# Ringless first stage, latent norms inside the projection loop and paced activation fetches in a two-block transformer kernel

## The reference, cut to what matters

```
mod = silu(c) @ w_ada + b_ada              # 48 columns of 128; the first 16 shift and scale h
h = rmsnorm(x) * (1 + sc_a) + sh_a
proj = h @ w_in                            # qa, ka, va, q_lat (256), kv_lat (128), k_rope (32)
q = rmsnorm(q_lat, q_norm) @ w_q_up        # latent attention, 8 heads
kv = rmsnorm(kv_lat, kv_norm) @ w_kv_up
...                                        # two attentions, w_out, residual
idx, g = the 16 best of 16384 experts per token and head
act = gelu(h @ expert_u[idx]);  x += g_f * sum(g * act * expert_v[idx])
```

## Time and profile before

| | us |
|---|---|
| median of 3 runs | 2427.87 (2425.49 to 2429.12) |
| profiled execution | 2450.04, span 2448.2, granted clock 0.98 |
| PE busy | 2336.0 (95%) |
| DVE, ACT, POOL busy | 1340.0, 784.0, 1079.8 |
| DMA | 409 MB, 167 GB/s over the span |

### The profile page before, as it was taken

One profiled execution on the slowest core, in us unless ns is written; L12 is line 12 of the kernel. 1 busy time (PEld: TensorE's weight loads), 2 busy tenths in 40 slices (PEclk: granted clock), 3 DMA queues, 4 the chain that ended last, 5 costly groups with the idle time before them and its releaser, 6 DMA issues. The chain is left out here.

```text
span 2448.2 us, 32933 instructions
## 1 busy us (share of the span) xinstructions
PE 2336.0 (95%) x11679; PEld 2001.3 (82%) x11679; DVE 1340.0 (55%) x2424; ACT 784.0 (32%) x1176; POOL 1079.8 (44%) x728
## 2 busy tenths in 40 slices
PE   6999998999999999999969999999999989999999
PEld 5777776888888888888759999999977767788787
DVE  5566656899763222222228888888866554333322
ACT  1344532222333222222213333333332442333211
POOL 0029653455788888884058877882100300000000
PEclk9999998999999999999979999999998999999999
DMA  6213226734577776677539999999721101223222
GB/s 249 69 55 111 80 92 232 241 129 148 126 177 197 142 145 143 148 143 214 188 117 331 349 355 357 369 345 350 287 80 48 35 18 61 86 95 99 92 88 88
DMA packets 177648, 409.03 MB, mean 167 GB/s; under 512 B 55712, under 2 KB 97568, under 8 KB 170528
## 3 DMA queue, kind: packets, MB, share of 16 engines
q1 hardware_dynamic: 115296, 315.53, 38.8%
q0 software_dynamic: 61696, 84.12, 13.4%
q10 hardware_dynamic: 576, 8.39, 1.0%
HBM read 347.00 MB, written 60.95 MB: 167 GB/s over the span
## 5 line engine op out<-in xcount | busy, mean ns | idle before, releaser
L1448 DVE TENSOR_TENSOR p_lo<-p_raw,p_hi 128x1024 fp32r<-128x1024 f32 x230 | 282.4, 1228 | 523.3 <-ACT p_hi L1347 374.4
L58 PE MATMUL ps<-p_h_hi,p_hi 128*128 128x512 f32 x1152 | 454.3, 394 | 8.2 <-DMA p_big<-keys_d 5.2
L59 PE MATMUL ps<-p_h_lo,p_hi 128*128 128x512 f32 x1152 | 449.8, 390 | 0.0
L60 PE MATMUL ps<-p_h_hi,p_lo 128*128 128x512 f32 x1152 | 449.8, 390 | 0.0
L1223 POOL DMA_INDIRECT gates<-p_tok,p_g_cell x256 | 410.5, 1603 | 78.3 <-issue 78.3
L58 PE MATMUL ps<-p_w_hi,p_hi 128*128 128x384 f32 x1024 | 347.4, 339 | 18.7 <-DVE p_w_lo L1596 14.6
L59 PE MATMUL ps<-p_w_lo,p_hi 128*128 128x384 f32 x1024 | 346.1, 338 | 4.2 <-issue 4.1
L60 PE MATMUL ps<-p_w_hi,p_lo 128*128 128x384 f32 x1024 | 346.2, 338 | 3.6 <-issue 3.6
L1347 ACT ACTIVATE p_hi<-p_raw 128x1024 fp32r<-128x1024 f32 x144 | 152.6, 1059 | 471.0 <-PE ps L60 464.9
L58 PEld LDWEIGHTS ps<-p_h_hi,p_hi 128*128 128x128 f32 x1152 | 217.4, 189 | 53.8 <-DMA p_big<-keys_d 5.3
L60 PEld LDWEIGHTS ps<-p_h_hi,p_lo 128*128 128x128 f32 x1152 | 217.0, 188 | 45.5
(11 more groups left out here) (361 smaller groups left out, 3890.8 us busy)
## 6 DMA issues: line engine op xcount, KB each, us to landing
p_raw<-U_d SPq DMA_DIRECT2D x128, 512.0 KB
p_raw<-V_d SPq DMA_DIRECT2D x128, 512.0 KB
a_w_raw<-w_ada_d SPq DMA_DIRECT2D x48, 512.0 KB, 3.9
activations<-p_q SPq DMA_DIRECT2D x128, 192.0 KB
f_raw<-w_gu_d SPq DMA_DIRECT2D x44, 512.0 KB, 3.5
gates<-p_dense POOLq DMA_DIRECT2D x16, 1024.0 KB, 8.2
p_big<-activations SPq DMA_DIRECT2D x8, 1536.0 KB
p_h_lo<-activations SPq DMA_DIRECT2D x8, 1536.0 KB
```

Of the source, the lines that this page charges most:

```text
L58: pe.matmul(out, w_hi, x_hi, start=start, stop=False)
L59: pe.matmul(out, w_hi, x_lo, start=False, stop=False)
L60: return pe.matmul(out, w_lo, x_hi, start=False, stop=stop)
L1448: dve.tensor_tensor(lo[:, r % 2, :], raw[:, r, :], hi[:, r % 2, :].bitcast(F32), ALU.subtract).then_inc(lo_ready, 1)
```

## The change

It has three parts. (1) First stage: the 16 `w_ada` blocks have places of their own in buffers that are free until later (`qh`, `kh`, `v_mla`, `q_swa`, `o_tok`), so SP waits for none of them. Seven blocks are raw, the last among them; nine are folded, and for five of these (`ADA_SCALED`) ACT makes the product with eight activations of 128x128, so that DVE only adds. PE's order is written out by hand, with the sums of squares after raw block 4; DVE inverts after its sixth fold; ACT's root stands behind the last scaled block. (2) The latent norms: sums after blocks KROPE and Q0, inverses at K and Q0+1, roots at K and Q0+1, the normed latents at Q0+2 and Q0+3, the key copy at Q0+1; `keep_awake(60)` goes. (3) peer: cells are fetched in groups of 8 with a ring of 4 groups; the first 16 are paced, two for each V tile; V tiles 4 and 5 are loaded before `group(1, 1)`.

```diff
-    ADA_RAW = [1, 4, 7, 9, 12, 14]
-    ADA_FOLD = [m for m in range(ADA_A) if m not in ADA_RAW]
+    ADA_RAW = [0, 2, 4, 9, 11, 14, 15]
+    ADA_FOLD = [1, 3, 5, 7, 6, 8, 10, 12, 13]
+    ADA_SCALED = [6, 8, 10, 12, 13]
+    SUMS_BY = 6
...
@@ sync
-                stream.loads(sp, 0, 2)
-                sp.dma_start(xT[:], xT_d).then_inc(x_loaded, 16)
-                stream.loads(sp, 2, 4)
+                for m in range(2):
+                    ada_load(m)
...
+                for m in range(2, 4):
+                    ada_load(m)
+                sp.dma_start(xT[:], xT_d).then_inc(x_loaded, 16)
+                for m in range(4, 10):
+                    ada_load(m)
+                stream.loads(sp, 0, 2)
+                for m in range(10, ADA_A):
+                    ada_load(m)
+                stream.loads(sp, 2, 4)
...
@@ gpsimd
-                pool.wait_ge(silu_done, 1)
+                pool.wait_ge(mod_step, 1)
...
@@ tensor
-                for m in ADA_RAW:
-                    ada(m)
+                ada(0)
+                ada(2)
                 pe.wait_ge(ones_in, 16)
+                column(0)
+                column(1)
+                keep_awake(pe, ps[:, 4, :], ones[:], 8)
+                ada(4)
                 for k in range(KD):
                     pe.wait_ge(norms.sq_ready, k + 1)
                     pe.matmul(norms.bank, ones[:], x_square(k), start=k == 0, stop=k == KD - 1).then_inc(norms.summed, 1)
-                for a, m in enumerate(ADA_FOLD):
-                    keep_awake(pe, ps[:, 4, :], ones[:], 2)
...
+                column(2)
+                column(3)
+                ada(9)
+                column(4)
+                column(5)
+                ada(11)
+                ada(14)
+                column(6)
+                ada(15)
+                for a in range(7, len(ADA_FOLD)):
+                    column(a)
                 keep_awake(pe, ps[:, 4, :], ones[:], 12)
...
-                    if j == K:
+                    if j == KROPE:
                         norms.sums(pe, ones[:], 1, KD, 2)
-                    if j == Q0 + 2:
-                        norms.sums(pe, ones[:], 2, KD + 2, 1)
...
-                keep_awake(pe, ps[:, 4, :], ones[:], 60)
+                    if j == Q0:
+                        norms.sums(pe, ones[:], 2, KD + 2, 1)
@@ scalar
+                def scale(b):
+                    m = ADA_SCALED[b]
+                    act.wait_ge(ada_in[m], 16)
+                    if b >= 2:
+                        act.wait_ge(multiplied, b - 1)
+                    for k in range(KD):
+                        ins = act.activation(scaled_w[b % 2][:, k, :], by_k(ada_w[m])[:, k, :], ACT.Copy, scale=cact[:, k:k + 1])
+                    ins.then_inc(prod_ready, 1)
...
+                scale(0)
+                scale(1)
                 stream.split_hi(act, 0)
                 stream.split_hi(act, 1)
+                scale(2)
+                scale(3)
+                scale(4)
                 norms.root(act, 0)
...
-                    if j == V:
+                    if j == K:
                         norms.root(act, 1)
+                    if j == Q0 + 1:
                         norms.root(act, 2)
+                    if j == Q0 + 2:
                         normed.act(act, KD, latn_hi, 2)
+                    if j == Q0 + 3:
                         normed.act(act, KD + 2, latn_hi[:, 2:3, :], 1)
+                    if j == Q0 + 1:
                         act.wait_ge(rotation.done, 1)
                         act.activation(kh[HD:MLA_QK, :, :], k_rope[HD:MLA_QK, :]...).then_inc(shared, 1)
@@ vector (the fold loop: a scaled block has the three adds alone; then)
+                    if a == SUMS_BY - 1:
+                        norms.inverse(dve, 0, KD, D)
...
-                    if j == Q0:
+                    if j == K:
                         norms.inverse(dve, 1, KD + 2, 2 * P)
-                    if j == V:
+                    if j == Q0 + 1:
                         norms.inverse(dve, 2, KD + 3, P)
+                    if j == Q0 + 2:
                         dve.wait_ge(norms.rstd_ready, 2)
...
+                    if j == Q0 + 3:
                         dve.wait_ge(norms.rstd_ready, 3)
...
@@ peer
-    FETCH = 16
+    FETCH, FETCH_RING = 8, 4
...
+                for t in range(4, 6):
+                    v_load(t, t % 4)
                 sp.wait_ge(projected, BLOCKS)
                 group(1, 1, True)
-                for t in range(4, 2 * GT):
+                for t in range(6, 2 * GT):
...
                 def fetch_cell(s):
+                    if s % FETCH == 0 and s // FETCH >= FETCH_RING:
+                        pool.wait_ge(slot_ready, s // FETCH - FETCH_RING + 1)
...
                 for s in range(2 * FETCH):
+                    if s % 2 == 0:
+                        pool.wait_ge(lo_ready, V0 + s // 2 + 1)
                     fetch_cell(s)
```

More of the change, by code:

```diff
@@ L89, in __init__ @@
         self.pooled = []
-        self.folded = []
         for n, (kind, _, _) in enumerate(items):
-            {"split": self.where, "raw": self.raws, "pooled": self.pooled, "folded": self.folded}[kind].append(n)
+            {"split": self.where, "raw": self.raws, "pooled": self.pooled}[kind].append(n)
     def wait_landed(self, eng, n):
@@ L588, in mixer1 @@
     QLAT, KVLAT, KROPE, K, Q0, V, UPQ, UPK, UPV, OUT = 0, 2, 3, 4, 5, 9, 10, 18, 22, 26
-    ADA_RAW = [1, 4, 7, 9, 12, 14]
-    ADA_FOLD = [m for m in range(ADA_A) if m not in ADA_RAW]
+    ADA_RAW = [0, 2, 4, 9, 11, 14, 15]
+    ADA_FOLD = [1, 3, 5, 7, 6, 8, 10, 12, 13]
+    ADA_SCALED = [6, 8, 10, 12, 13]
+    SUMS_BY = 6
     ADA_POOL = list(range(ADA_A, 48))
[L594 to L597, removed]
+    items = [("split", w_in_d[m], SLOT) for m in range(10)]
     items += [("split", w_q_up_d[m], SLOT) for m in range(2)] + [("split", w_kv_up_d, SLOT)]
@@ L627, in mixer1 @@
                                                             sem("ada_done"))
+        ada_in = [sem(f"ada_in{m}") for m in range(ADA_A)]
+        raw_done, multiplied, prod_ready = sem("raw_done"), sem("multiplied"), sem("prod_ready")
         fold_step, fold_ready, fold_done = sem("fold_step"), sem("fold_ready"), sem("fold_done")
@@ L634, in mixer1, with by_k @@
         k_pads = [k_swa[:], o_tok[:, 1, 1, :]]
-        fold = qh[:, 0:2, :].rearrange("p a (k c) -> p (a k) c", c=P)
-        folded = qh[:, 2:5, :].rearrange("p a (k c) -> p (a k) c", c=P)
+        ada_w = [h[:, 2 * i:2 * i + 2, :] for h, n in ((qh, 4), (kh, 4), (v_mla, 2), (q_swa, 2)) for i in range(n)]
+        ada_w += [o_tok[:, i // 2, 2 * (i % 2):2 * (i % 2) + 2, :] for i in range(4)]
+        def by_k(block):
+            return block.rearrange("p a (k c) -> p (a k) c", c=P)
+        fold = by_k(normed.full[:])
+        scaled_w = [product[:], by_k(normed.x[:])]
+        folded = [h[:, c * P:c * P + P] for h in (k_swa[:], v_swa[:].rearrange("p t c -> p (t c)")) for c in range(4)]
+        folded += [partial[:, c, :] for c in range(2)]
         ss = sb("ss", [P, 2 * TT])
         def x_square(k):
-            return o_tok[:, k // TT, k % TT, :]
+            return norms.sq[:, k, :] if k < 2 else rotation.x[:, k - 2, :] if k < 4 else rotation.t[:, (k - 4) // 2, k % 2, :]
         square = rotation.t[:, 1, 1, :]
@@ L669, in _, with ada_load @@
             def _(sp):
+                def ada_load(m):
+                    sp.dma_start(ada_w[m], w_ada_d[m].rearrange("p (a n) -> p a n", a=2)).then_inc(ada_in[m], 16)
                 sp.dma_start(cols[:], cols_d).then_inc(cols_in, 16)
-                stream.loads(sp, 0, 2)
-                sp.dma_start(xT[:], xT_d).then_inc(x_loaded, 16)
-                stream.loads(sp, 2, 4)
+                for m in range(2):
+                    ada_load(m)
                 o, w = TABS["ones"]
                 sp.dma_start(ones[:], tabs_d[:, o:o + w]).then_inc(ones_in, 16)
-                stream.loads(sp, 4, ADA_A + 2)
+                for m in range(2, 4):
[7 more added lines that the diff above has]
+                stream.loads(sp, 2, 4)
                 sp.dma_start(sink[:], sink_d).then_inc(loaded, 16)
@@ L680, in _ @@
                     sp.dma_start(dst[:], tabs_d[:, o:o + w]).then_inc(loaded, 16)
-                stream.loads(sp, ADA_A + 2)
+                stream.loads(sp, 4)
             @block.gpsimd
@@ L712, in ada, with column @@
                         return
-                    n = stream.raws[ADA_RAW.index(m)]
-                    stream.wait_landed(pe, n)
+                    pe.wait_ge(ada_in[m], 16)
                     for k in range(KD):
-                        mm = pe.matmul(ps[:, 6, m:m + 1], stream.raw[:, n % stream.R, k * P:k * P + P], cact[:, k:k + 1],
+                        mm = pe.matmul(ps[:, 6, m:m + 1], by_k(ada_w[m])[:, k, :], cact[:, k:k + 1],
                                        start=(k == 0), stop=(k == KD - 1))
-                    mm.then_inc(stream.raw_used, 1)
```

(39 more changed lines are left out.)

8 lines of the change are left out of this document (3 added, 5 removed).

## The result

The changed kernel takes 2400.49 us (median of 4 runs, 2394.37 to 2404.01) against 2426.68 (2413.72 to 2429.12) for the kernel before: ratio 0.99, 95% interval 0.9859 to 0.9942. It is 26 us faster. The time lies inside the range, 28 us above the forecast; the gain is a little less than half of the 55 that were summed. The profiled execution takes 2404.01, span 2402.2.

The account below looks back on a forecast made before the run. PE was taken to bound the kernel, busy 95% of the span, partly with useless matmuls, and waiting at V's start. 15 + 13 + 27 = 55 off the profiled 2450.0 gives 2395, less 22.2 gives 2373; range 2362 to 2402.

Parts of the forecast that it names:

- The median of the runs is 22.2 lower; the same difference gives 2373: Whole kernel: profiled 2450.0 less 55 gives 2395; the profile-to-median difference of 22.2 was then subtracted to reach 2373.
- Part 1: First stage: PE still sets its end, first useful matmul moves from 61.92 to 46.8; gain 15, bounds 21 and 7.
- Part 2: Latent norms in the projections: 15.7 + 2 - 3 - 1 - 1 = 13 gained; bounds 16 and 5.
- waits before V: Projections: inverse at Q0+1, then ACT's root and key copy, delay block V's inputs; a new PE wait of about 3.
- the wait before block 5: Projections, at 96.81: ACT was held in the third square; with the sums one block earlier the wait goes, gaining 2.
- Behind V the third latent and the last split take 1 more: Projections, between block V and UPQ: finishing the latents was charged as a loss of 1.
- Part 3: Start of V: 29.1 lost up to tile 7's end; pacing cells recovers all but 2; gain 27, bounds 31 and 0.
- Rival 1: Start of V: the stall comes from entering loops, not the cells; gain 28 + 0 to 4, about 2398; chance 0.17.
- what is late is its code: Start of V: matmuls inside a tile wait for no semaphore, so PE's waits of up to 1.77 are for late code.
- Rival 2: Early norms become waits of 3 each at K, Q0+1, Q0+2; total gain 47, 2381; chance 0.16 shared with Rival 3.
- Rival 3: First stage: PE fills it, unloading DVE is beside the path; gain 7 there, total 47, 2381; 0.16 shared with Rival 2.
- Rival 4: V: rows come late because POOL sets the pace above 3.84 a pair; 99 lost at 5.0, about 2440; chance 0.04.

Follow-up runs that it names:

- A: Comparison on one chip: kernel before 2453.02, again 2453.92; only the peer edits 2426.08; changed kernel with peer as before 2435.06; 64 cells at once 2496.31.
- C: Comparison on another chip: kernel before 2452.43; changed kernel 2406.29; only the peer edits 2422.52; changed kernel with peer as before 2430.64; 64 cells at once 2490.47.
- E: Comparison on another chip: kernel before 2456.23; with cells paced in groups of 8, old load order, 2425.47; with only V tiles 4 and 5 loaded earlier 2459.15.
- B: Comparison on another chip: kernel before 2426.24, again 2421.99; changed kernel 2403.47; with the key copy later 2398.73; with useless matmuls moved besides 2400.29.
- D: Comparison on another chip: kernel before 2422.92; only the peer edits 2422.76; only the load order 2423.11; 64 cells 2459.8; later key copy with moved useless matmuls 2398.21.
- with the copy later: Changed kernel with ACT's copy of the rotated key at Q0+2 instead of Q0+1: 2398.73, against 2403.47 for the changed kernel beside it.
- E's pair: Kernel before with only V tiles 4 and 5 loaded earlier, 2459.15, and with only groups of 8 and pacing, 2425.47; the kernel before took 2456.23.
- bursts of 64: Kernel before with FETCH 32 instead of 16, so 64 cells at once instead of 32: ratios 1.0176, 1.015 and 1.0149 in three comparisons.
- pacing alone: Kernel before with cells in groups of 8, the ring and the first 16 paced, load order as before: 2425.47 against 2456.23.
- second kernel of the last experiment: Changed kernel with the key copy at Q0+2, 16 useless matmuls behind V and 6 instead of 12 before the first pair: 2400.29, ratio 0.9891.

## Why the prediction was right and wrong

**The sum.** The step that failed is "The median of the runs is 22.2 lower; the same difference gives 2373". It took the 22.2 us between the profiled execution and the median as a constant that lies outside the change. By all that the runs show they were the stall itself: the kernel before stalls for about 30 us on chips A, C and E and not on B and D, and its profile (2450.04, with the stall) belongs to the first kind (2452 to 2456), its median (2427.87) to the second (2423 to 2426). Which chips these two were taken on isn't known. Against its own kind the sum is 9 us off, by C: 2452.43 - 2406.29 = 46 for 55. On the other kind part 3 has nothing to remove, and the sum would have been 28 for the 23 and 26 measured. The sign in the text was there: an execution 22 us above runs that agreed within 4 us (2425.49 to 2429.12), where the same text found a stall of 29.

**Part 1**, forecast 15, first useful matmul at 46.8: 48.69, 45.24 and 46.60 in the three profiles, so 13 to 17. Right, and in its reason: PE-bound, one raw block fast, useless matmuls 5.47 for 5.8, a scaled block 2.43 for 2.4. Root done at 40.0, forecast 38.4.

**Part 2**, forecast 13: 116.2 - 109.6 = 6.6, and 2.2 in a second profile, where PE runs block V at half rate (granted clock 0.50 for the 19 us from 109.7). The terms for the waits before V (3) and the useless matmuls gone were right. Of the 2 for the wait before block 5 only 0.6 shows, at a granted clock of 0.87 from 62 to 75 us, against 1.00 before; with the copy later and 1.00 there it is 2.5. Mis-sized was "Behind V the third latent and the last split take 1 more": 4.10, and another 2.4 for twelve matmuls at half rate (12 x 0.2). The durations were taken from rows in which DVE ran alone; POOL's products now fall beside more of DVE's norms. From 111.42 to 125.8 DVE is busy without a pause, and its instructions beside POOL's take 4.9 us longer in all than alone, an estimate from the rows of both kernels: as much as the whole wait. The Trainium skill (SBUF — State Buffer, section 🔬 SBUF: two separate sides) says that VectorE and GpSimd share a port pair that one instruction holds to its end while the other blocks; the rows agree (0.49 becomes 2.13 when POOL's 1.90 begins first). That would have been the term to add.

**Part 3**, forecast 27 in the profile of before: 64.65 - 33.6 = 31 in the profiles, 27, 30 and 31 in time on A, C and E. Right where the stall is; 0 on D. Rival 1 (the stall is not from the cells) is refuted by E's pair; its gain of 28 is near what was measured, but by the wrong road. The prediction's own step "what is late is its code" is not borne out: no packet of the instruction queues moves in the stall. The Trainium skill (DMA: Bandwidth & Descriptors, section SWDGE vs HWDGE vs iDMA) says that SP's transfers never touch the path on which GpSimd makes its descriptors. The rows agree for the data: of ACT's waits in the stall 36.8 us are "remote" and none is for a load of V.

**The rivals.** Rival 2 (waits at K, Q0+1 and Q0+2, part 2 gives 5) came near the size of part 2 with the places wrong: the waits stood before V and before UPQ, none at K. Its own terms add up to 7, not 5. Rival 3 did not occur. Rival 4 did not occur in the changed kernel, and its mechanism was seen with bursts of 64 on D, where it cost 37. Its price in the text doesn't add up: 99 lost on top of 2373 is 2472, not 2440.

**Open:** what differs between the two kinds of chip, and whether it is the chip. Five were seen, each in one comparison, three with the stall and two without, and no profile shows a cause. Open too is how the burst holds PE and ACT.

## What to carry to other kernels

Before a stall from one profiled execution is counted as a gain, set that execution beside the timed runs: if it is longer by about the stall, the stall may not be in the runs at all, and both sums must stand in the range. A long burst of small GpSimd transfers is better paced: here it held PE and ACT where they enter a loop, on three chips of five, and with 64 cells it stood ahead of rows that were soon due. A duration taken from a row where an engine ran alone grows when the change puts GpSimd's elementwise work beside VectorE.

## What the runs showed of the hardware that was not expected

The same kernel differs by about 29 us between chips (2425 and 2454, the means of its medians on two and on three) through one stall, and by a second amount within a chip. The two windows are the second 60 us behind V of the changed kernel and of pacing alone:

```profile
1807.00:1867.00 60.00, 56.19 (x232) 46.11 (x231) 39.27 (x36) 12.40 (x18) 10.29 (x8) 0.80 0.15 49
```

```profile
1830.00:1890.00 60.00, 53.43 (x265) 40.93 (x264) 43.81 (x46) 17.45 (x27) 19.94 (x16) 1.00 0.20 66
```

The first has a granted clock of 0.80, the second 1.00, and the kernel ends 656.5 us after V's last matmul in the first and 644.5 in the second, from the same code. The second kernel of the last experiment on B shows it too: a profiled run of 2379.47 with 1.00 there, a median of 2400.29. Of the 20 profiles 17 have the lower clock; what decides is open, and some 12 us would be there for whoever finds it.
